# State space layer tile by tile inside the prompt attention's steps, and the GLU with the second decode batch behind it

## The reference, cut to what matters

```
h = RMSNorm(x)*(1+scale1)+shift1 ; z = h @ W_in        # columns q | k | v | u, 512 each
att = dilated window attention, 8 heads of 64           # prompt: 512 x 512; decode: cached keys and values
ssm: bu = B u ; h = scan(a, bu) ; y = Re(C h) + D u     # 32 groups x 64 complex states
     y = gelu(y) ; y = (y @ glu_a) * sigmoid(y @ glu_b)
x = x + g1 * (concat(RMSNorm(att), RMSNorm(ssm)) @ W_out)
x = x + g2 * moe(RMSNorm(x)*(1+scale2)+shift2)          # 4 groups of 4 experts, top 1 and top 2
out = RMSNorm(x), the new k and v, the last states
```

## Time and profile before

| | |
|---|---|
| median of 3 runs | 889.87 us |
| profiled execution | 890.12 us, its span 888.3 us |
| TensorE, VectorE, ScalarE, GpSimd busy | 82%, 33%, 19%, 19% of the span |
| chain that ended last | TensorE 72%, VectorE 9%, DMA 5%, GpSimd 5% |
| DMA | 212.06 MB, mean 239 GB/s |

### The profile page before, as it was taken

One profiled execution on the slowest core, in us unless ns is written; L12 is line 12 of the kernel. 1 busy time (PEld: TensorE's weight loads), 2 busy tenths in 40 slices (PEclk: granted clock), 3 DMA queues, 4 the chain that ended last, 5 costly groups with the idle time before them and its releaser, 6 DMA issues.

```text
span 888.3 us, 10288 instructions
## 1 busy us (share of the span) xinstructions
PE 732.8 (82%) x3994; PEld 423.3 (48%) x3994; DVE 292.1 (33%) x753; ACT 165.8 (19%) x384; POOL 167.5 (19%) x258
## 2 busy tenths in 40 slices
PE   1499999998999967767899736999999999999700
PEld 1286588885556554643445523434434443443200
DVE  3723222542334267542246362111111011111038
ACT  1331000042324231222122100011011011111032
POOL 1225210004870016552000001000000000000073
PEclk8588999998799968899899756999999999999955
DMA  9970298257636360824424694866979999999352
GB/s 319 382 263 5 79 292 301 96 200 274 254 120 259 98 270 1 337 91 84 157 77 149 235 315 166 307 237 254 399 289 402 404 397 397 402 396 401 137 201 100
DMA packets 83127, 212.06 MB, mean 239 GB/s; under 512 B 3516, under 2 KB 9948, under 8 KB 80997
## 3 DMA queue, kind: packets, MB, share of 16 engines
q1 hardware_dynamic: 69254, 179.89, 55.0%
q0 software_dynamic: 5472, 19.16, 6.3%
q10 hardware_dynamic: 8352, 12.34, 4.1%
HBM read 197.18 MB, written 17.86 MB: 242 GB/s over the span
## 4 chain that ended last, share of the span: by engine, by line
PE 72%; DVE 9%; DMA 5%; POOL 5%; issue 3%; SPq 2%; ACT 2%; ACTq 0%; POOLq 0%; DVEq 0%
PE ps L2294 19%; PE ps L2297 12%; PE ps L1950 10%; PE ps L2204 6%; PE ps L1830 5%; PE ps L1919 3%; DMA toeplitz<-g_d 2%; PE ps L1983 2%; PE ps L1981 2%; PE ps L1843 2%; SPq L529 2%; DMA ring<-in_w_out 2%; PE ps L2001 1%; PE ps L2044 1%; POOL yg L782 1%
## 5 line engine op out<-in xcount | busy, mean ns | idle before, releaser
L2294 PE MATMUL ps<-ering,xgT 128*128 128x512 f32 x256 | 115.5, 606 | 2.5 <-ACT xgT L799 1.7
L1950 PE MATMUL ps<-hT,ring 128*128 128x272 f32 x384 | 88.8, 393 | 0.0
L1950 PEld LDWEIGHTS ps<-hT,ring 128*128 128x128 f32 x384 | 72.7, 190 | 15.4 <-issue 0.6
L2294 PEld LDWEIGHTS ps<-ering,xgT 128*128 128x128 f32 x256 | 48.7, 194 | 63.7 <-issue 60.4
L2297 PE MATMUL ps<-ering,xgT 128*64 128x512 f32 x320 | 70.7, 595 | 1.2 <-ACT xgT L799 1.2
L766 POOL DMA_INDIRECT xg<-h_d,gidx x13 | 12.3, 949 | 243.3 <-PE ps L1830 210.6
L2294 PE MATMUL ps<-ering,aT 128*128 128x512 f32 x128 | 56.2, 593 | 0.0
L1843 PE MATMUL ps<-ring,silu_c 128*32 128x128 f32 x768 | 27.5, 309 | 24.5 <-DMA ring<-in_ada_w 24.5
L2297 PEld LDWEIGHTS ps<-ering,xgT 128*64 128x64 f32 x320 | 22.6, 137 | 44.7 <-issue 43.3
L1743 DVE SCALAR_TENSOR_TENSOR a_t<-a_t,ps 128x512 f32<-128x512 f32 x13 | 8.9, 688 | 97.2 <-ACT a_t L799 97.2
L1843 PEld LDWEIGHTS ps<-ring,silu_c 128*32 128x32 f32 x768 | 24.9, 125 | 26.9 <-issue 17.5
(11 more groups left out here) (434 smaller groups left out, 1074.7 us busy)
## 6 DMA issues: line engine op xcount, KB each, us to landing
ering<-in_w_gate SPq DMA_DIRECT2D x16, 2048.0 KB, 17.5
ering<-in_w_up SPq DMA_DIRECT2D x16, 2048.0 KB, 16.9
ering<-in_w_down SPq DMA_DIRECT2D x16, 2048.0 KB, 21.1
ring<-in_ada_w SPq DMA_DIRECT2D x12, 2048.0 KB, 12.9
ring<-in_cache_k SPq DMA_DIRECT2D x8, 1792.0 KB, 10.9
ring<-in_cache_v SPq DMA_DIRECT2D x8, 1792.0 KB, 11.5
ring<-in_w_in SPq DMA_DIRECT2D x4, 2048.0 KB, 22.3
y_d<-ysb ACTq DMA_DIRECT2D x26, 256.0 KB, 6.1
```

The source lines that it names most:

```text
L1950: ins = mm(out, r[:, 512 * k + P * c:512 * k + P * (c + 1)], hT[:, k, cols], start=k == 0, stop=k == KD - 1)
L2294: return mm(out, lhsT=lhs, rhs=ering[slots[0]][:, cols], start=k == 0, stop=k == n - 1)
```

## The change

The loop over 2-tile groups is gone. Each of the 16 tiles t now has fixed places in the attention's steps: `s5_in` in step 2t+1, rotation and scans in 2t+2, `s5_out` in 2t+4, square and cubic in 2t+5, tanh and `gelu_out` in 2t+6. The last tile's parts lie behind step 31. `probs_t` and `pv` have one PSUM bank each (2 and 3), the state space layer has banks 4 and 5. On VectorE `head_out` is split: the reciprocal stands ahead of the state space part of a step, the multiplication behind it. The GELU works in `u4`.

`chat` is built in the projection, before `mod_chunk` 5 to 8 in GpSimd's order; `tmat` behind the last u chunk, before `mod_chunk` 9 to 11. The loads of `ct_re` and `ct_im` are issued right behind the zeroing of `y_d`. VectorE waits ahead of the attention for the landing of the conditioning stores.

Behind the attention stand the four transposes, tokens and GLU, with the second decode batch between them; `wo(0, 0)` is ahead of `dec_values`.

```diff
+IN_AT = {2 * t + 1: t for t in range(STT)}
+SCAN_AT = {2 * t + 2: t for t in range(STT)}
+OUT_Y_AT = {2 * t + 4: t for t in range(STT)}
+SQUARE_AT = {2 * t + 5: t for t in range(STT)}
+GELU_AT = {2 * t + 6: t for t in range(STT)}
+LAST_STEP = 2 * STT + 6
...
# SyncE
-        sp.wait_ge(s("bu"), NGR)
+        sp.wait_ge(s("bu"), STT)
...
-        sp.wait_ge(s("hout"), NGR + 1)
+        sp.wait_ge(s("hout"), STT + 1)
...
-        sp.wait_ge(s("yp"), NGR)
+        sp.wait_ge(s("yp"), STT)
# GpSimd
+        pool.wait_ge(s("btTe"), 9)
+        pool.wait_ge(s("gst"), 16)
+        for b, n in enumerate(("ct_re", "ct_im")):
+            pool.dma_start(ct2[b][:, :, :], I[n]).then_inc(s("h0"), 16)
...
         pool.sem_inc(s("padt"), 1)
-        for c in range(N_EARLY + 1, N_ADA):
-            mod_chunk(c)
...
+        pool.wait_ge(s("h0"), 32)
         for m in range(TDEC):
...
+        for c in range(N_EARLY + 1, N_ADA - 3):
+            mod_chunk(c)
+        pool.wait_ge(s("z"), 24)
+        for b, n in enumerate(("h0_re", "h0_im")):
+            pool.dma_start(h0[:, b, :, :], I[n]).then_inc(s("h0"), 16)
+        o(pool.memset(tmat[:, :, :], 0.0))
+        for j in range(TDEC):
+            for i in range(j, TDEC):
+                m = TDEC - 1 - (i - j)
+                o(pool.tensor_copy(tmat[32 * j:32 * j + 32, :, 32 * i:32 * i + 32], kmat[32 * m:32 * m + 32, :, :]))
...
+        for c in range(N_ADA - 3, N_ADA):
+            mod_chunk(c)
...
+        for t in range(STT):
+            b = t % 2
+            cs, sn = [a[:, t, 0:NCK - 1].unsqueeze(1).broadcast_to([P, 2, NCK - 1]) for a in (cosT, sinT)]
+            g, h, q = sg[b][:, :, 0:NCK - 1], Hs[b][:, :, 1:NCK], hp[:, :, 1:NCK]
+            pool.wait_ge(s("scan"), t + 1)
+            if t >= 2:
+                pool.wait_ge(s("yp"), t - 1)
+            pool.tensor_tensor(h, g, cs, ALU.mult)
+            o(pool.tensor_tensor(q, g, sn, ALU.mult))
+            pool.tensor_tensor(h[:, 0, :], h[:, 0, :], q[:, 1, :], ALU.subtract)
+            pool.tensor_copy(gl[:, t:32:16], sg[b][:, :, NCK - 1])
+            pool.tensor_copy(Hs[b][:, :, NCK:N4], h0[:, :, t, :])
+            o(pool.tensor_tensor(h[:, 1, :], h[:, 1, :], q[:, 0, :], ALU.add))
+            pool.sem_inc(s("hout"), 1)
# ScalarE, in step st between the exp and the copy of the transposed probabilities
+        def gelu_square(t):
+            act.wait_ge(s("yp"), t + 1)
+            if t >= 2:
+                act.wait_ge(s("gel"), t - 1)
+            f(u4[:, t, :], ps[:, 5, 0:N4], ACT.Copy).then_inc(s("ycp"), 1)
+            f(gy[t % 2][:, :], ps[:, 5, 0:N4], ACT.Square, scale=float(np.sqrt(0.044715))).then_inc(s("ysq"), 1)
+        def gelu_tanh(t):
+            act.wait_ge(s("gin"), t + 1)
+            f(gy[t % 2][:, :], gy[t % 2][:, :], ACT.Tanh, scale=float(np.sqrt(2.0 / np.pi))).then_inc(s("gth"), 1)
...
+            gelu_step(st)
             act.wait_ge(s("pt"), st + 1)
# VectorE
+        def rotate(t):
+            cs, sn = [a[:, t, :].unsqueeze(1).broadcast_to([P, 2, NCK]) for a in (cosT, sinT)]
+            w = ps[:, 4, 0:2 * N4].rearrange("p (a b) -> p a b", a=2)
...
+            dve.wait_ge(s("bu"), t + 1)
+            tt_(rx[:, :, :], w[:, :, 0:NCK], cs, ALU.mult)
+            tt_(rt_[:, :, :], w[:, :, 0:NCK], sn, ALU.mult)
+            v.tensor_copy(sw[:, :, t, :], w[:, :, NCK:N4]).then_inc(s("buread"), 1)
+            dve.wait_ge(s("buread"), t + 1)
+            tt_(rx[:, 0, :], rx[:, 0, :], rt_[:, 1, :], ALU.add)
+            tt_(rx[:, 1, :], rx[:, 1, :], rt_[:, 0, :], ALU.subtract).then_inc(s("xadd"), 1)
...
+        def gelu_cubic(t):
+            dve.wait_ge(s("ycp"), t + 1)
+            dve.wait_ge(s("ysq"), t + 1)
+            a = gy[t % 2][:, :]
+            stt(out=a, in0=a, scalar=1.0, in1=u4[:, t, :], op0=ALU.add, op1=ALU.mult).then_inc(s("gin"), 1)
...
+        for b in (1, 2):
+            dve.wait_ge(s_modst[b], 64)
         for st in range(NST + 2):
             if st < NST:
                 row_max(st)
+            if st >= 2:
+                inverse_sum(st - 2)
+            s5_step(st)
             if st >= 2:
                 head_out(st - 2)
...
+        for st in range(NST + 2, LAST_STEP + 1):
+            s5_step(st)
+        dve.wait_ge(s("gel"), STT)
         for j in range(QT):
             att_out(j)
# TensorE
-            if st >= 2:
-                pe.wait_ge(s("ptr"), st - 1)
+            if st:
+                pe.wait_ge(s("ptr"), st)
...
-            if st >= 2:
-                pe.wait_ge(s("att"), st - 1)
+            if st:
+                pe.wait_ge(s("att"), st)
...
+        for st in range(NST + 2, LAST_STEP):
+            s5_step(st)
+        dec_keys(1, 0)
+        dec_keys(1, 1)
         for j in range(QT):
             att_t(j)
+        s5_tokens(0)
+        dec_keys(1, 2)
+        s5_glu(0, 0)
+        s5_tokens(1)
+        s5_glu(0, 1)
+        dec_keys(1, 3)
+        s5_glu(1, 0)
+        s5_tokens(2)
+        s5_glu(1, 1)
+        s5_sum(0)
+        dec_probs_t(1)
+        s5_glu(2, 0)
+        s5_tokens(3)
+        s5_glu(2, 1)
+        s5_sum(1)
+        s5_glu(3, 0)
+        wo(0, 0)
+        s5_glu(3, 1)
+        s5_sum(2)
+        for part in range(4):
+            dec_values(1, part)
+        s5_sum(3)
```

More of the change, by code:

```diff
@@ L263, in _build @@
     dq = small("d_by_tile", 16)
-    gla, gli = small("g_last_re", 16), small("g_last_im", 16)
+    gl = small("g_last", 32)
     las, lai = small("last_re", 16), small("last_im", 16)
@@ new lines, in _ @@
+        gla, gli = gl[:, 0:16], gl[:, 16:32]
+        lc, ls = cosT[:, :, NCK - 1], sinT[:, :, NCK - 1]
+        pool.tensor_tensor(las[:, :], gla, lc, ALU.mult)
+        pool.tensor_tensor(lai[:, :], gla, ls, ALU.mult)
+        o(pool.tensor_tensor(ctmp[:, :], gli, ls, ALU.mult))
+        o(pool.tensor_tensor(gli, gli, lc, ALU.mult))
+        o(pool.tensor_tensor(las[:, :], las[:, :], ctmp[:, :], ALU.subtract))
+        o(pool.tensor_tensor(lai[:, :], lai[:, :], gli, ALU.add))
+        pool.sem_inc(s("hout"), 1)
@@ L1033, in _ @@
             w = TW[j]
-            wo_a(p)
             if p:
+                wo_a(p)
                 h2T_half(p - 1)
@@ L1409, in dec_out, with scans, gelu_out, s5_step @@
                 op0=ALU.mult, op1=ALU.mult).then_inc(s("dOe"), 1)
+        def rotate(t):
+            cs, sn = [a[:, t, :].unsqueeze(1).broadcast_to([P, 2, NCK]) for a in (cosT, sinT)]
+            w = ps[:, 4, 0:2 * N4].rearrange("p (a b) -> p a b", a=2)
+            if t:
+                dve.wait_ge(s("scan"), t)
+            dve.wait_ge(s("bu"), t + 1)
[5 more added lines that the diff above has]
+            tt_(rx[:, 1, :], rx[:, 1, :], rt_[:, 0, :], ALU.subtract).then_inc(s("xadd"), 1)
+        def scans(t):
+            b = t % 2
+            dve.wait_ge(s("xadd"), t + 1)
+            if t >= 2:
+                dve.wait_ge(s("hout"), t - 1)
+            m = mag4[:, t:t + 1].broadcast_to([P, NCK])
+            v.tensor_tensor_scan(sg[b][:, 0, :], m, rx[:, 0, :], 0.0, ALU.mult, ALU.add)
+            v.tensor_tensor_scan(sg[b][:, 1, :], m, rx[:, 1, :], 0.0, ALU.mult, ALU.add).then_inc(s("scan"), 1)
+        def gelu_cubic(t):
[3 more added lines that the diff above has]
+            stt(out=a, in0=a, scalar=1.0, in1=u4[:, t, :], op0=ALU.add, op1=ALU.mult).then_inc(s("gin"), 1)
+        def gelu_out(t):
+            dve.wait_ge(s("gth"), t + 1)
+            stt(out=u4[:, t, :], in0=gy[t % 2][:, :], scalar=1.0, in1=u4[:, t, :], op0=ALU.add, op1=ALU.mult)\
+                .then_inc(s("gel"), 1)
+        def s5_step(st):
+            if st in SCAN_AT:
+                rotate(SCAN_AT[st])
+            if st in SQUARE_AT:
+                gelu_cubic(SQUARE_AT[st])
+            if st in SCAN_AT:
+                scans(SCAN_AT[st])
+            if st in GELU_AT:
+                gelu_out(GELU_AT[st])
+        for b in (1, 2):
+            dve.wait_ge(s_modst[b], 64)
         for st in range(NST + 2):
@@ L2053, in dec_probs_t, with s5_in, s5_out, s5_step @@
             tr(ps[0:NS, b0 + 1, 3 * P:4 * P], dP[:, CK:DK]).then_inc(s("dPt"), 1)
+        def s5_in(t):
+            if t:
+                pe.wait_ge(s("buread"), t)
+            for n in range(2):
+                ins = mm(ps[:, 4, N4 * n:N4 * (n + 1)], bt[n][:, t, :], u4[:, t, :], start=True, stop=True)
+            ins.then_inc(s("bu"), 1)
+        def s5_out(t):
+            pe.wait_ge(s("hout"), t + 1)
+            if t == 0:
+                pe.wait_ge(s("chat"), 1)
+            else:
+                pe.wait_ge(s("ysq"), t)
+            out, h = ps[:, 5, 0:N4], Hs[t % 2]
+            mm(out, tmat[:, t, :], u4[:, t, :], start=True, stop=False)
+            mm(out, chat[0][:, t, :, :].rearrange("p a b -> p (a b)"), h[:, 0, :], start=False, stop=False)
+            mm(out, chat[1][:, t, :, :].rearrange("p a b -> p (a b)"), h[:, 1, :], start=False, stop=True)\
+                .then_inc(s("yp"), 1)
+        def s5_step(st):
+            if st in IN_AT:
```

(5 more changed lines are left out.)

374 lines of the change are left out of this document (90 added, 284 removed).

## The result

The changed kernel takes 910.31 us (median of 4 runs, 907.0 to 914.39) beside 890.93 for the kernel before on the same chip: ratio 1.0214, 95% interval 1.0169 to 1.0259. It is slower by some 19 us. The forecast was 894 with a range of 876 to 909, so the direction was the likelier one and the time lies just outside. In some executions, of the kernel before too (13 of 25 beside a3_one_bank_each, which does it itself in five of ten), the time is some 904 us in place of 890; medians take these in, ratios leave out what lies over 1.5% above the fastest of the same kernel.

The account below looks back on a forecast made before the run. It took the stretch from attention's end to w_out's product, 113 us and ended by SyncE's queue, as the one to shorten. 16.8 + 4.5 + 22 - 39 = +4.3 on 890.12 gave 894, 8 in 10 within 876 to 909.

Parts of the forecast that it names:

- Part 3, middle: Projection: chat, behind late C loads, delays mod_chunk(5) and its store, so TensorE stands 14.3 us and restarts cold: +16.8 us.
- Rival 1: Projection: the C loads arrive early, chat hides and TensorE does not stall: 878 us, chance 0.17.
- Part 3, late: Projection's end: mod_chunks 9 to 11 wait behind tmat, so last store and first exp come later: +4.5 us, 3 to 7.
- Part 2, attention: Attention: state space products add 18.8 us, 2 fill idle, 5 come from waits and locks: +22 us, 14 to 36.
- my 4 us: Attention: value products wait for head_out behind VectorE's state space work, 0.7 us for some six heads.
- rival 3: Attention: VectorE's order becomes the bound as rotation and scans are locked out, growth 36: 908 us, chance 0.15.
- the even steps' length: Attention: even iterations with rotate, scans and gelu_out take 3.4 us, heads 12.4 against TensorE's 11.7.
- Part 1, tail: From attention's end to the product of w_out's second half: 74 us where it was 113, gain 39, bounds 30 to 44.
- A' to t0: From the attention's last written head to the issue of the second batch's cache_v: 21 us, 19 to 26.
- the last cover: Tail: the sample rows' turn ends near 51 us after cache_v's issue, hidden behind w_out's landing at 53.
- Rival 4: Tail gives less: w_out still queued behind mod3, cold restart, slow stretch before cache_v's issue: 906 us, chance 0.10.
- rival 2: Attention fills better, growth 14, and the stretch from its end to cache_v's issue is warm at 19: 884 us, chance 0.13.

Follow-up runs that it names:

- a3_one_bank_each: Kernel before, with only the attention's PSUM banks changed to one each for transposed probabilities and value products, state space work unmoved: 898.30 us, ratio 1.0065.
- m1: Changed kernel, with GpSimd issuing the two C loads ahead of the y_d zeroing instead of behind it: 890.59 us, ratio 0.9959 to the kernel before.
- l2: Changed kernel, with VectorE's wait for the conditioning stores' landing moved from before its first row maximum to before its first head_out: 903.47 us, ratio 1.0127.
- l1: Changed kernel, with GpSimd doing mod_chunk 9 to 11 ahead of the tmat memset and copies: 900.08 us, ratio 1.0083 to the kernel before.
- a1: Changed kernel, with VectorE's first decode softmax in step 13 instead of 14 and the probabilities' copy in 19 instead of 18: 903.20 us, ratio 1.0123.
- c2: Changed kernel with mod_chunk 5, 6 and 9 to 11 earlier, decode softmax in step 13, its copy in 19, w_out's first half ahead of cache_v: 870.29 us.
- c4: c2 with VectorE's gelu_cubic one step after ScalarE's square, tanh and gelu_out one step later too: 872.00 us, ratio 0.9774 to the kernel before.

## Why the prediction was wrong, step by step

- **Part 3, middle (+16.8; measured +18.2).** Right in mechanism and size. The chat block took 31.4 us; I had 28.7 and 3 for VectorE's table work beside it, and the last of its instructions indeed went from 1.27 to 1.58. TensorE's idle was 15.3 against 14.3. Rival 1, the early C loads, fell with the trace: the C loads took 27.0 us behind the zeroing, and m1 shows 6.7 ahead of it. The Trainium skill (DMA: Bandwidth & Descriptors, Queues, rings and completion order) has each DMA engine take a ring's descriptors in ring order, in a paragraph on the queues of SyncE and ScalarE; these two runs agree with it for GpSimd's queue.
- **Part 3, late (+4.5; measured +9.2).** The store was as late as I had it (235.97 less 18.2 is 217.8, I said 218). Two steps behind it failed. The larger is "ScalarE then has its k and v stores and a table load to do, some 7": these took 10.3 us (235.97 to 246.31), as v's last store alone took 7.40 to issue, against 7.3 and 4.43 in the kernel before. The other is "VectorE's new wait, for the stores' landing, ends about then too": the landing took 12.21 us among the cache loads, and the first exp came 2.5 us behind ScalarE's queue, which is what l2 takes back. Besides, my own times, 225.5 less 221.40, make 4.1 and not 4.5. l1 recovers 8.75 us.
- **Part 2, attention (+22; measured +31.3).** This is the largest miss, and what failed is that the sum had no term for the clock: time at the low level went from 11 to 27 us, which costs 7.9 us of the 9.3 missing. About 10 us of this time follow the stall of step 15. The rest of the sum was near: at the full clock the attention grew by 23.3 (114.3 less 91.0). TensorE's busy time rose by 20.6 (113.51 in a1 less 92.95) where I had 18.8, its idle time by 1.9 (5.5 in a1 less 3.6) where I had 5 less 2. The mechanism behind my 4 us is in the traces: TensorE waits for `head_out` 4.0 us in a1 and in c2, where I had 0.7 in some six heads, and 2.3 us in the changed kernel, whose stall of step 15 takes the place of some of these waits. It needs both halves of the change: one bank each without the state space work costs under 1 us (a3). The lock-out of rival 3 is not in the attention, where GpSimd starts behind the scans: these took 0.42 and 0.40 us in place of 0.58 and 0.55. That the two halves of the sum at the full clock come so near is in part luck, 1.8 too little on one and 1.1 too much on the other. I had looked for trouble in the even steps' length, not in the one step where the decode softmax meets rotation, scans and `gelu_out` ahead of a four-block row maximum.
- **Part 1, tail (-39; measured -40.2).** A' to t0 18.9 us (21), first half of w_out at t0+26.1 (24), its product 9.3 us (9), w_out issued at t0+44.4 (43), second product at A'+72.8 (74). Only the last cover was wrong: w_out landed at 447.7 and the sample rows' turn ended the wait, not the load. Rival 4 fell, and rival 2 with the attention's growth. Behind 449.43 there are 2.2 us more, a stretch that I moved whole; what makes them stays open.
- Rival 3 forecast 908, near the truth by another road: it wanted attention longer by VectorE's lock-outs, and c4 and the scans' times say no.

With the three measured terms in place of mine (18.2, 9.2, 31.3) the same sum gives 910. The 16.4 us between 4.3 and the measured 20.7 are thus 9.3 in the attention, 4.7 late, 1.4 in the middle and 2.2 at the end, less 1.2 in the tail.

## What to carry to other kernels

- Ask of each engine's program, when work moves forward in it, which small instruction now stands behind it: 0.45 us of addition behind 31 us of multiplication cost 18 us, and swapping them cost nothing that the traces show.
- A load issued behind a long transfer in the same queue is as late as that transfer; put the short one that someone waits for ahead.
- Compare stages by length times granted clock as well as by length. The first tells what work was added, the second what the clock did with it; a saving seen in one trace can be nearly all clock, as 8.4 of a1's 8.8 us were.
